# Query projection and last feed in token halves, value turns beside the last latent, and low parts awaited one slab at a time

## The reference, cut to what matters

```
n = rmsnorm(x, g_mix); z = n @ w_in
qa, ka, va, qi, ki, wi, cq, ckv, kr, ga, gb = split(z)
score = einsum(relu(einsum(qi, ki)), wi * idx_scale)     # 4 index heads of 64
sel = top_k(where(causal, score, -inf), 256)
y_a = attention(qa, ka[sel], va[sel], alibi)
q_b = rmsnorm(cq, g_cq) @ w_uq ; kv = rmsnorm(ckv, g_ckv) @ w_ukv     # ranks 384 and 256
y_b = causal_attention(rope(q_b), [k_nope, rope(kr)], v)
h = x + (sigmoid(ga) * (y_a @ w_pa) + sigmoid(gb) * (y_b @ w_pb)) @ w_out
h = h + square(relu(rmsnorm(h) @ w_ff1)) @ w_ff2
h = h + sigmoid(rmsnorm(h, g_ple) @ w_ple_gate) * (p @ w_ple)
out = rmsnorm(h, g_final)
```

## Time and profile before

| what | us |
| --- | --- |
| median of 3 runs | 1735.89 |
| lowest, highest | 1733.52, 1736.64 |
| the profiled execution | 1734.33 |
| its span in the trace | 1732.5 |
| TensorE busy | 1645.8 (95%) |
| VectorE busy | 1171.8 (68%) |
| ScalarE busy | 690.0 (40%) |
| GpSimd busy | 636.1 (37%) |

### The profile page before, as it was taken

One profiled execution on the slowest core, in us unless ns is written; L12 is line 12 of the kernel. 1 busy time (PEld: TensorE's weight loads), 2 busy tenths in 40 slices (PEclk: granted clock), 3 DMA queues, 4 the chain that ended last, 5 costly groups with the idle time before them and its releaser, 6 DMA issues.

```text
span 1732.5 us, 22637 instructions
## 1 busy us (share of the span) xinstructions
PE 1645.8 (95%) x8344; PEld 1287.3 (74%) x8344; DVE 1171.8 (68%) x1826; ACT 690.0 (40%) x1139; POOL 636.1 (37%) x397
## 2 busy tenths in 40 slices
PE   5899989999999999999999899999999999999997
PEld 4658778787755666667888777888878888888786
DVE  7349999990335566655434766776689999998335
ACT  5342232322255566651124433434354444444223
POOL 2212342221210000022211544445479888886221
PEclk9999999999999999999999999999999999999999
DMA  5201113224300010002443143344387445521112
GB/s 156 82 21 35 55 49 97 87 96 119 78 1 1 2 51 24 2 1 73 146 158 133 49 157 135 134 166 169 134 287 272 159 143 176 180 86 61 43 55 97
DMA packets 110342, 171.92 MB, mean 99 GB/s; under 512 B 18752, under 2 KB 68928, under 8 KB 110240
## 3 DMA queue, kind: packets, MB, share of 16 engines
q1 hardware_dynamic: 106400, 156.93, 27.3%
q10 hardware_dynamic: 3680, 13.63, 2.1%
q0 software_dynamic: 160, 0.02, 0.0%
HBM read 121.14 MB, written 47.58 MB: 97 GB/s over the span
## 4 chain that ended last, share of the span: by engine, by line
PE 84%; DVE 8%; ACT 3%; issue 2%; DMA 2%; POOL 1%; SPq 0%; ACTq 0%; DVEq 0%; POOLq 0%
PE ps L2064 34%; PE ps L2451 16%; PE ps L2410 14%; PE ps L2295 3%; PE ps L2309 3%; PE ps L2260 2%; PE ps L2279 2%; PE ps L2266 2%; PE ps L2174 2%; PE ps L2122 2%; PE ps L2135 1%; DMA hid_scratch<-t_out 1%; PE ps L2374 1%; DVE prob_a L1737 1%; PE ps L2236 1%
## 5 line engine op out<-in xcount | busy, mean ns | idle before, releaser
L947 POOL TENSOR_TENSOR w_lo<-w_raw,w_hi 128x1024 fp32r<-128x1024 f32 x67 | 165.7, 2475 | 526.8 <-ACT w_hi L1096 526.8
L1015 POOL TENSOR_TENSOR a_lo<-s_raw,a_hi 128x512 fp32r<-128x512 f32 x128 | 188.5, 1480 | 94.9 <-ACT a_hi L1339 94.0
L1096 ACT ACTIVATE w_hi<-w_raw 128x1024 fp32r<-128x1024 f32 x67 | 70.8, 1060 | 358.6 <-PE ps L2064 311.6
L2064 PE MATMUL ps<-n_hi,w_hi 128*128 128x512 f32 x576 | 181.6, 397 | 17.1 <-POOL w_lo L947 4.6
L2410 PE MATMUL ps<-b_hi,a_hi 128*128 128x512 f32 x448 | 177.3, 396 | 10.2 <-ACT u_two L1397 4.4
L2064 PE MATMUL ps<-n_lo,w_hi 128*128 128x512 f32 x576 | 180.0, 394 | 0.0
L2064 PE MATMUL ps<-n_hi,w_lo 128*128 128x512 f32 x576 | 180.0, 394 | 0.0
L2451 PE MATMUL ps<-b_hi,a_hi 128*128 128x512 f32 x448 | 174.4, 389 | 2.4 <-DVE h L1957 2.4
L2410 PE MATMUL ps<-b_lo,a_hi 128*128 128x512 f32 x448 | 175.9, 393 | 0.0
L2410 PE MATMUL ps<-b_hi,a_lo 128*128 128x512 f32 x448 | 175.9, 393 | 0.0
L1015 POOL TENSOR_TENSOR a_lo<-f_raw,a_hi 128x512 fp32r<-128x512 f32 x96 | 137.0, 1441 | 105.6 <-ACT a_hi L1339 105.5
(11 more groups left out here) (314 smaller groups left out, 3141.9 us busy)
## 6 DMA issues: line engine op xcount, KB each, us to landing
f_raw<-in_w_ff_dram SPq DMA_DIRECT2D x64, 512.0 KB, 4.5
b_lo<-hid_scratch SPq DMA_DIRECT2D x112, 256.0 KB, 5.5
hid_scratch<-c_out SPq DMA_DIRECT2D x32, 512.0 KB, 5.0
w_raw<-in_w_in_dram SPq DMA_DIRECT2D x28, 512.0 KB, 3.6
hid_scratch<-t_out SPq DMA_DIRECT2D x15, 768.0 KB, 6.9
gates_scratch<-stage ACTq DMA_DIRECT2D x16, 512.0 KB, 2.7
sig_ab<-gates_scratch SPq DMA_DIRECT2D x8, 1024.0 KB, 6.0
x_tok<-in_x_dram SPq DMA_DIRECT2D x8, 512.0 KB, 10.2
```

What stands on the lines that cost most here:

```text
L947: pool.tensor_tensor(lo_of(first)[:, :, :], w_raw[s][:, :, :], hi_of(first)[:, :, :].bitcast(F32), ALU.subtract).then_inc(lo_ready, 1)
L1015: pool.tensor_tensor(slot(a_lo, o), first_of(o), slot(a_hi, o).bitcast(F32), ALU.subtract).then_inc(a_lo_done, 1)
L1096: act.activation(hi_of(first)[:, :, :], w_raw[s][:, :, :], ACT.Copy).then_inc(hi_ready, 1)
L2064: last = pe.matmul(bank(4 * half + 2 * j + t)[0:w, :], wm, xm[:, t * HALF:(t + 1) * HALF], start=(n == 0 and a), stop=(n == total - 1 and ...
```

## The change

- The turns of tiles 4 to 7 alternate between banks 4-5 and 6-7. The qi projection is made by token halves: first half of the tokens in banks 0 and 2, its step k = 0 ahead of the last turn, then the second half. SP loads its slabs among the x tiles, ACT splits them behind x_hi of tiles 4 and 5.
- ACT copies `ki`, DVE `wi` and `kr`. Two qa_steps stand ahead of the turns of `wi`, twelve between the units of index scores and two behind them. ACT's order around the two Sin operations is changed.
- Four projects run in a row behind the index; the value turns go into the last latent's group, as its second tile. ACT copies `va` behind the last latent. POOL makes low parts between `latent_lo`'s split and its sum.
- Keys of B run with k outermost and wait for one slab at a time. DVE writes two of the last four value tiles. An empty group keeps the parity of the halves.
- Feed 2 goes ahead of gate project 3. The last feed runs by token halves with a signal after the first (`feed_first`), and the last gate and its sigmoid go by halves too.

```diff
@@ sync
             for t in range(1, TT):
                 sp.dma_start(x_tok[:, t, :], ...)
+                if t == TT - 4:
+                    load(wt(wi, 0, KT, QI0, WCOL))
+                if t == TT - 3:
+                    load(wt(wi, KT, KT, QI0, WCOL))
-            load_kn(wi, QI0)
...
             for q in range(1, 2 * OUT_N):
+                if q == 2 * OUT_N - 1:
+                    load_feed(q - 1)
                 load_kn(pg, q * WCOL)
-                load_feed(q - 1)
-            load_feed(2 * OUT_N - 1)
+                load_feed(q - 1 if q < 2 * OUT_N - 1 else q)
@@ gpsimd
-            def latent_lo(c):
+            def latent_lo(c, slabs=0):
                 pool.tensor_tensor(dst_lo, full, dst_hi, ALU.subtract)
+                lo_parts(slabs)
...
-            latent_lo(2)
+            latent_lo(2, 1)
             latent_lo(3)
-            lo_parts(2)
+            lo_parts(1)
             latent_lo(4)
@@ scalar
                 if t >= 1:
                     x_hi(t - 1)
-            hi_parts(2)
+                if TT - 3 <= t < TT - 1:
+                    hi_parts(1)
             x_hi(TT - 1)
...
-            act.activation(ki_wi[HEAD_DIM:P, :], tile_ps(half, 0)[HEAD_DIM:P, :], ACT.Copy).then_inc(ki_out, 1)
...
+            half, _, _, free = at_.group(2)
+            for j, part in enumerate((slice(0, HALF), slice(HALF, S))):
+                act.wait_ge(gate_in, q + 2 + j)
+                act.activation(tmp[:, q % 2, :, part], tmp[:, q % 2, :, part], ACT.Sigmoid).then_inc(gate_fn, 1)
@@ vector
+            dve.tensor_copy(ki_wi[HEAD_DIM:P, :], tile_ps(half, 0)[HEAD_DIM:P, :]).then_inc(ki_out, 1)
...
+            for j in range(2, 4):
+                dve.tensor_scalar(vb[:, 4 + j, :], bank(4 * half + j), kv_norm[:, 4 + j:5 + j], None,
+                                  ALU.mult).then_inc(vb_dve, 1)
@@ tensor
+                if t == X_WHOLE:
+                    freed(pe, 1, 2)
+                if t > X_WHOLE + 1:
+                    freed(pe, t % 2, t // 2)
...
+            for t in range(TT - 1):
+                turn_x(t)
             pe.wait_ge(inv_copied, 1)
-            project()
+            qi_part(0, range(0, 1))
+            turn_x(TT - 1)
+            qi_part(0, range(1, DT))
+            qi_part(1, range(DT))
             project(((0, P),))
...
+            qa_step(0)
+            qa_step(1)
...
-                if 1 <= u <= 2 * DT:
-                    qa_step(u - 1)
+                if u in QA_AT:
+                    qa_step(2 + QA_AT.index(u))
+            qa_step(2 * DT - 2)
+            qa_step(2 * DT - 1)
             pe.wait_ge(rel_done, 2 * len(IDX_UNITS))
-            for _ in range(3):
+            for _ in range(4):
                 project()
             half = group()
             for t in range(TT):
-                last = pe.transpose(bank(4 * half, 2)[:, t * P:(t + 1) * P], va_features[:, t * P:(t + 1) * P], ident[:, :])
-            last.then_inc(turn_done, 1)
-            project()
-            project(((0, P),))
+                pe.transpose(tile_ps(half, 1)[:, t * P:(t + 1) * P], va_features[:, t * P:(t + 1) * P], ident[:, :])
+            product(half, ((0, P),), (KT, KT), normed)
...
             for g in range(2):
                 half = group()
-                for j in range(2):
-                    for k in range(KVT):
+                for k in range(KVT):
+                    if g == 0:
+                        pe.wait_ge(lo_ready, kv_slabs[k][2] + 1)
+                    for j in range(2):
...
-            for q in range(1, 2 * OUT_N):
-                project(moving=residual)
-                feed()
+            project(moving=residual)
+            feed()
+            project(moving=residual)
             feed()
+            feed()
+            project(moving=residual)
+            last_feed()
```

More of the change, by code:

```diff
@@ L1130, in _ @@
             hi_parts(1, 2)
+            half = group(2)
+            act.activation(qi[:, :, :].rearrange("q a n -> q (a n)"), bank(4 * half, 4), ACT.Copy).then_inc(
+                psum_free[half], 1)
             act.wait_ge(rope_arg, 2)
@@ L1200, in _ @@
             latent_hi(1, half)
-            half = group()
-            act.activation(va[:, :, :].rearrange("q t n -> q (t n)"), bank(4 * half, 2), ACT.Copy).then_inc(
-                psum_free[half], 1)
             hi_parts(2)
@@ L1267, in _ @@
                 half = group(2 * g)
-                for j in range(4):
+                for j in range(4 if g == 0 else 2):
                     t = 4 * g + j
                     last = act.activation(vb[:, t, :], bank(4 * half + j), ACT.Copy, scale=kv_norm[:, t:t + 1])
-                last.then_inc(psum_free[half], 1)
+                if g == 0:
+                    last.then_inc(psum_free[half], 1)
+                else:
+                    last.then_inc(vb_act, 1)
+                    act.wait_ge(vb_act, 1)
+                    act.wait_ge(vb_dve, 2)
+                    act.sem_inc(psum_free[half], 1)
+            act.sem_inc(psum_free[at_.group()[0]], 1)
+            at_.turns -= 1
             hi_parts(2)
@@ L1994, in take_gate @@
                     dve.wait_ge(h_final, 2 * (q - 1))
[L1995 to L2007 removed]
+                parts = [slice(0, S)] if q < 2 * OUT_N - 1 else [first, second]
@@ new lines, in take_gate @@
+                for part in parts:
+                    for t in range(2):
+                        last = part.stop == S and t == 1
+                        dve.tensor_tensor(tmp[:, q % 2, t, part], tile_ps(half, t)[:, part], rms[:, part],
+                                          ALU.mult).then_inc(psum_free[half] if last else gate_in, 1)
+            def take_feed(q):
+                whole = q < 2 * OUT_N - 1
+                half, done, _, _ = at_.group(1)
+                if whole:
+                    complete(dve, done)
+                for part in [slice(0, S)] if whole else [first, second]:
+                    gate = tmp[:, q % 2, :, part]
+                    if not whole:
+                        if part.start == 0:
+                            dve.wait_ge(feed_first, 1)
+                        else:
+                            complete(dve, done)
+                    dve.wait_ge(gate_fn, q + 1 + (part.start != 0))
+                    if whole:
+                        dve.tensor_tensor(gate, gate, ps[:, 4 * half:4 * half + 4, :].rearrange(
+                            "q (a t) n -> q a (t n)", a=2), ALU.mult).then_inc(psum_free[half], 1)
@@ L2011, in take_feed @@
+                        dve.wait_ge(fed, 2 if part.stop < S else 3)
                     for j in range(2):
@@ L2105, in _ @@
[L2105 to L2109 removed]
+            filled = at_.groups // 2
             qa_slabs = [at_.slab() for _ in range(DT // KT)]
@@ L2240, in _ @@
                     last.then_inc(turn_done, 1)
+            at_.group()
+            at_.turns -= 1
             for half in range(2):
```

143 lines of the change are left out of this document (96 added, 47 removed).

## The result

The changed kernel takes 1692.05 us (median of four runs, 1689.31 to 1698.0) against 1735.48 for the kernel before beside it: a ratio of 0.9759, 95% interval 0.9732 to 0.9785. The profiled execution took 1689.66 us, its span is 1687.9, and the mean granted clock 0.996 (before 0.982).

The account below looks back on a forecast made before the run. TensorE, 95% busy, was taken as the bound: its work, idle time and clock. Gains of 0.4, 10.3, 6.1, 7.5, 4.6, 1.2 and 2.5 sum to 32.6 us; 1734.33 less these, plus 1.56, gives 1703.3 us, range 1699 to 1713.

Parts of the forecast that it names:

- Index and latents: Index scores, latents and first gates: TensorE's waits and the low clock behind them go, 10.3, 6.1 and 7.5 us.
- Keys of B: Keys of B: the 3.8 us wait becomes two short ones and the clock holds, gain 4.6 us; 2.7 if not.
- values: Last values of B: copies shared by ACT and DVE take 1.2 us instead of 2.42, gain 1.2.
- end: Last feed: DVE adds the first half while TensorE makes the second, gain 2.5 of a 2.6 us wait.
- Start: Last turns and qi: gain 1.1 us, or -0.8 if the clock stays low behind turn 7; 0.4 taken.
- a rigid chain of TensorE work that shifts as a whole: Everything between the changed places: TensorE's work only moves earlier, with no gain or loss of its own.
- the attention's start clock: Start of attention: the clock there might give 2 us more, counted only in the range's low end.
- the 15 us that DVE had to spare: Norm group at about 417 us: DVE's reciprocal is ready at 376, TensorE needs it after 391.
- A: Remaining or other waits: the clock falls all the same, taking back 9 us, 1712 us; chance 0.2.
- B: First gate slab's low part or ki's second slab: a margin of 1 to 2 us is missed, 1708; chance 0.18.
- C: Long dense stages: the chip grants less clock and the kernel is slower, 1758 us at 0.95; chance 0.03.
- D: Start and end: the token halves give nothing, the rest does, 1706 us; included in the main case's 0.57.

Follow-up runs that it names:

- p_start: Only the start's part of the change (token-half query projection, turns 4 to 7 alternating banks, slabs among x tiles) on the kernel before: 1730.88 us, ratio 0.9985.
- p_end: Only the end's part of the change (feed 2 ahead of gate project 3, last gate and feed by halves) on the kernel before: 1730.69 us, ratio 0.9984.
- v_start: Changed kernel with turn 4 in banks 6-7, turn 5 in 4-5, and the two slab splits each ahead of an x split: 1692.87, 1692.86 and 1691.51 us.

## Why the prediction was wrong

The sign was right, and so were the mechanisms in the index, the latents, the keys, the values and the end; the time was below the range. The miss of the median is 11.3 us (1692.05 for 1703.3). Of it 1.9 is the base, 7.1 the gain (39.7 for 32.6, the forecast had four fifths of it), and 2.3 luck: the four executions have the median 1692.05, all 19 the mean 1694.3. That mean, too, is below 1699.

- *Index and latents*: 24.3 measured for 23.9 (10.3 + 6.1 + 7.5). The first score came at 70.95, 4.2 behind the end of ki (forecast 4.4); the waits for relu, for ACT's cq and for the low part went, and the 384 behind the scores took 87.04, so the clock behind them came back as priced.
- *Keys of B* 4.7 for 4.6; *values* 0.9 for 1.2, the rest of the wait being 1.6 where about 1.3 was named; *end* 2.6 for 2.5 (81.92 for 360 in a row, then no wait ahead of the last turns).
- *Start*: the one term of the sum that was clearly mis-sized, 3.0 (stages) or 2.6 (alone) for 0.4. The forecast had qi end at 57.1; it ended at 55.82. The turns came when they were expected. But it priced turn 7 at 1.94 and the six matmuls ahead of it at 2.7; they took 1.23 and, from the turn before (ended 31.81) to turn 7, 2.36. So turn 7 no longer ran at the low rate, and the 90 behind it took 20.42, the full rate. And the forecast took the old start's loss from one profile, 1.88, where the profiles with the old start had 1.8 to 3.1 (144 in 34.42 to 35.79), 2.5 in the mean. Of the 2.6 missing, 0.7 is the discount from 1.1 to 0.4 for a clock that stays low, 1.3 the earlier end of qi, 0.6 the old start's mean.
- *"What lies between these places is a rigid chain of TensorE work that shifts as a whole"*: this is the step that failed. It put the unchanged stages at nothing. The work shifted, but its clock wasn't rigid. The waits for ya_lo, u_two and sq_sum stayed, at or near their old length, and in the six profiles these stages cost 6.9 us less (some 4 to 5 over all executions, by the estimate above): 1.5 up to the first of them, 1.2 from there to the MLP's 984 matmuls, 4.2 from these to the last norm (2.6 by the 984, 1.6 by the four matmuls behind sq_sum, both with the low clock before and without it after). Why the clock fell less there stays open. The forecast's range let "the attention's start clock" give 2 and nothing else; a low end that let the clock vary at each remaining wait would have reached 1692 (1699 less the 6.9).
- *The base*: the forecast stood on a median of three, 1735.89, by adding 1.56 to the profiled run; many runs gave 1734.0, which makes 1.9 of the miss.
- *A slip that cost nothing*: the forecast has TensorE shift by about 26 us ahead of the norm group, where its own terms up to there give 24.3. The profiles have 27.3 at the queries (423.5 to 396.2), still inside the 15 us that DVE had to spare.

Of the rivals: A (the clock doesn't come back) is refuted behind the index scores, at the gates and at the keys (384 in 87.04, 432 in 97.95, 36 in 8.50); its other half, that it falls at other waits, was so in two of four profiles, at 300, 455 and 750 us, and still without 1712. B is refuted by the margin of 0.97 met at POOL, C by stretches at the full rate (384 in 87.04, 984 in 223.31, where the granted clock is 1.00 from 1010 to 1230 us), D by p_start and p_end, 2.6 and 3.0.

The Trainium skill's rule that I weighed (TensorE: Matmul & The Clock Gate, section PE-mode transpose), that the full clock does not engage for transposes, doesn't describe this case: eight transposes took 1.94 in most places, 1.23 behind six matmuls in the changed kernel and 1.09 behind a wait of 1.76 us in v_start, where TensorE had done nothing but transposes since four tiny matmuls at 6.37 us. Two stretches of v_start, columns as above, hold eight transposes in 1.09 at a granted 1.00 and eight in 1.94 at 0.50:

```profile
21.00:22.30 1.30, 1.09 (x8) 0.85 (x8) 1.30 (x3) 1.27 (x4) 0.00 (x0) 1.00 0.07 28
27.00:29.00 2.00, 1.93 (x9) 1.96 (x10) 1.86 (x3) 1.97 (x4) 0.00 (x0) 0.50 0.55 99
```

In the changed kernel's profile the granted clock reads 1.00 from 27 to 35 us although its six matmuls stand 0.43 us apart there, so in this early part the pace tells the level and the granted clock doesn't. With the rule I gave the start -0.8; the runs say 2.6 to 3.0.

## What to carry to other kernels

Price a removed wait at its length plus what the clock costs behind it, and make the range wide enough for the clock at the waits that stay: here it moved the same program by 6 us from one execution to the next. Walk the feeding engine's queue to the tenth of a microsecond where a wait hangs on it: placing one 2.4 us operation second instead of fourth was worth 5 us. Take the base from as many executions as there are, and put a delay meant as a probe where no wait stands close behind it.

## What the runs showed of the hardware

- Behind the same wait of the same program, the same work ran at a granted clock of 1.00 in some executions and at a lower one in others (384 matmuls in 87.34 or 88.96, 432 in 98.22 or 99.78, 1.6 us each). Over all the kernels here the MLP's 984 took one of few times, 223.3 to 223.5, 224.7 to 224.9 or 225.8 to 226.1.
- TensorE's transposes of 128 x 128 fp32 ran at both levels of the clock, eight in 1.94 at a granted 0.50 or in 1.09 at 1.00 (v_start).
- DVE's two-input operation of 128 x 1024 took 1.92 and 2.00 beside POOL's subtraction of the same size, 1.28 at the end of the kernel where POOL was idle (the changed kernel, from 1673.69).
